# Attention units with 128 keys: the scaling of the probabilities goes from VectorE to ScalarE

## The chip, the cores and the metric

One core of a Trainium2 chip. The kernel is one program, written by hand for each engine with semaphores between them. The metric is device time in microseconds (us) of one execution; the median of three runs of the kernel before is 2493.39 us (2491.39 to 2496.73).

## What is computed

Two transformer blocks one after the other, on 256 tokens of width 1024 in float32. Their mixers hold several attentions, all of them with the same softmax. Cut to what the change touches:

```python
def masked_softmax(s, mask):
    s = jnp.where(mask, s, NEG_INF)
    m = jnp.max(s, axis=-1, keepdims=True)
    p = jnp.where(mask, jnp.exp(s - m), 0.0)
    return p / jnp.maximum(jnp.sum(p, axis=-1, keepdims=True), TINY)
...
    # nsa_attention, 16 heads of 64: three attentions, each weighted by a gate per token and head
    o = gc[..., 0:1] * o_c + gc[..., 1:2] * o_s + gc[..., 2:3] * o_w
```

DSA and MoBA (8 heads of 64 each) and MLA (8 heads of 192, values of 128) have no gate. All of these are causal: the first 128 queries see at most 128 keys, the second 128 queries see up to 256. The memory attention (4 heads of 128) has 256 keys for every query.

## The kernel before, in words

Everything lies in SBUF (on-chip memory) in one big array (`arena` in the profile); weights come by DMA in slabs through a ring, and TensorE multiplies them with activations of 256 tokens. Between the big products stand the attention stages. The list `units` holds their work: one unit is a pair of heads (e = 0, 1) for one block of 128 queries (`qt`), with `nk` keys. The order is: MoBA (8 units), DSA (8), memory attention (4), NSA in three kinds of 16 units each (kind 0 with 15 compressed keys, kinds 1 and 2 with 128 or 256 keys), memory attention (4), MLA (8): 80 units. In MoBA, DSA, NSA kinds 1 and 2, and MLA the even units have 128 keys and the odd ones 256; 28 units have 128 keys, and 16 of these, those of NSA, have a gate.

A unit u goes through these steps, in a software pipeline written out once per engine (`attention` in the block of each engine; the loop index is i):

- TensorE `scores(u)` writes query times key to PSUM (`pair`, a pair of banks). In round i it does `scores(i + 1)`, then `between` (in MoBA/DSA and NSA one or two products of the memory attention's weights, `memory_products`), then `values(i - 3)`, then `turn_p(i - 2)`. In MLA, where nothing is between, `turn_p(i - 2)` stands ahead of `values(i - 3)`.
- VectorE `maxima(u)`: L1699 scales and masks the scores (PSUM to `pb` in SBUF) and frees the scores' bank, L1704 takes the negative maximum. L1699 waits for the scores of u and, since `pb` has three places, for `turn_p(u - 3)` (semaphore `pT_done`).
- ScalarE `probs(u)`, L1215: the exponential of each head with the row sum as a second output (an ACTIVATE and an ACTIVATION_READ_ACCUMULATOR for each head).
- VectorE `weights(u)`: L1710 takes the reciprocal of the two sums, then a TENSOR_SCALAR for each head multiplies the probabilities by it (L1714), or by it and by the gate (L1716).
- TensorE `turn_p(u)`, L831: transposes the probabilities to the one PSUM bank there is for this (in MLA there are two), so it also waits for `copy_p(u - 1)`.
- ScalarE `copy_p(u)`: L1227 for 256 keys, L1230 for 128, takes the transposed probabilities to SBUF.
- TensorE `values(u)` (under L543, the line of every ordinary matmul), then VectorE `outputs(u)`, L1726 (adds to what is there) or L1728.

Each engine runs its own instructions in order, so a wait holds up everything behind it. ScalarE's order in a round is `probs(i)`, `copy_p(i - 2)`, `between` (L1207, `memory_out`: a copy of a finished memory product, for which TensorE waits before it starts the next group). VectorE's order is `maxima(i)`, `weights(i - 1)`, `outputs(i - 4)`, and in MoBA a round of the top-k of DSA (L2039, L2042).

Of the kernel before, what the change touches and what calls it, by code (L numbers as in the profile page):

```python
# [8 lines left out]
ALU = mybir.AluOpType  # L9
ACT = mybir.ActivationFunctionType  # L10
# [3 lines left out]
P = 128  # L14
# [4 lines left out]
HD = 64  # L19
# [186 lines left out]
def build(nc, stream, adaw_d, crow_d, xin, memin, cols_d, rows_d, gmrows_d, gmws_d, cmpw_d, consts_d, pos_d, out_d):  # L206
    with ExitStack() as ctx:
# [17 lines left out]
        stat = sb("stat", [P, 7, 56])  # L225
# [15 lines left out]
        def sem(name):  # L241

            if name not in sems:
                sems[name] = ctx.enter_context(nc.semaphore(name))
            return sems[name]
# [96 lines left out]
        def nsa_units(kind):  # L342
            def make(pair, qt):
                g = pair // 2
                gate = [stat[:, 5 + qt, 3 * (2 * pair + e) + kind:3 * (2 * pair + e) + kind + 1] for e in range(2)]
                if kind == 0:
                    return dict(qt=qt, nk=N_CMP, scale=HD ** -0.5, mask=cmpmask[:, qt, 0:N_CMP], gate=gate, dv=HD,
                                s=[[(qT[HD * e:HD * e + HD, pair, qt * P:qt * P + P],
                                     kcmpT[HD * e:HD * e + HD, g * N_CMP:g * N_CMP + N_CMP])] for e in range(2)],
                                v=[[vcmp[0:N_CMP, g, :]]] * 2, out=oT[:, pair, qt * P:qt * P + P], add=False)  # L350
                nk = P * (qt + 1)
                keys, v0 = (kT, NS_VS) if kind == 1 else (kwT, NS_VW)
                return dict(qt=qt, nk=nk, scale=HD ** -0.5, mask=causal[:, qt, 0:nk], gate=gate, dv=HD,
                            s=[[(qrT[HD * e:HD * e + HD, pair, qt * P:qt * P + P],
                                 keys[HD * e:HD * e + HD, g, 0:nk])] for e in range(2)],
                            v=[[tm[:, kt, v0 + HD * g:v0 + HD * g + HD] for kt in range(qt + 1)]] * 2,
                            out=oT[:, pair, qt * P:qt * P + P], add=True)
            return make
# [24 lines left out]
        U_MEM1 = add_units("mem1", 2, mem_unit)  # L383
        U_MLA = add_units("mla", 4, mla_unit)


        def pair_jobs(c0, n, dst, d0):

# [150 lines left out]
        def _(pe):  # L539
# [265 lines left out]
            def attention(first, last_unit, between=None):  # L805
                behind = 1 if between is None else 0

                def scores(u):
                    un = units[u]
                    if u >= 2:  # L810
                        pe.wait_ge(sem("scores_read"), u - 1)
                    for e in range(2):
                        parts = un["s"][e]
                        for i, (q, k) in enumerate(parts):
                            ins = mm(spair[u % 2][:, e, 0:un["nk"]], q, k, i == 0, i == len(parts) - 1)
                    ins.then_inc(sem("scores_done"), 1)

                def turn_p(u):
                    un = units[u]
                    nk = un["nk"]  # L820
                    pe.wait_ge(sem("p_done"), u + 1)
                    if u > behind:
                        pe.wait_ge(sem("pT_copied"), u - behind)
                    tb = banks[TB[u % 2 * behind]]
                    if nk < P:
                        for e in range(2):
                            ins = mm(tb[0:nk, e * TOK:e * TOK + P], pb[:, u % 3, e, 0:nk], ident, True, True)
                    else:
                        for e in range(2):
                            for kt in range(nk // P):  # L830
                                ins = nc.tensor.transpose(tb[:, (2 * e + kt) * P:(2 * e + kt + 1) * P],  # L831
                                                          pb[:, u % 3, e, kt * P:kt * P + P], ident)
                    ins.then_inc(sem("pT_done"), 1)

                def values(u):
                    un = units[u]
                    kp = min(un["nk"], P)
                    pe.wait_ge(sem("pT_copied"), u + 1)
                    if u >= 2:
                        pe.wait_ge(sem("o_read"), u - 1)  # L840
                    ob = banks[OB[u % 2]]
                    for e in range(2):
                        vs = un["v"][e]
                        out = ob[HD * e:HD * e + HD, 0:P] if un["dv"] == HD else ob[:, e * P:e * P + P]
                        for kt, v in enumerate(vs):
                            ins = mm(out, v, pT[0:kp, u % 2, 2 * e + kt, :], kt == 0, kt == len(vs) - 1)
                    ins.then_inc(sem("o_done"), 1)

                scores(first)
                for i in range(first, last_unit + 3):  # L850
                    if i + 1 < last_unit:
                        scores(i + 1)
                    if between is not None:
                        between(i - first)
                    if behind and first <= i - 2 < last_unit:
                        turn_p(i - 2)
                    if i - 3 >= first:
                        values(i - 3)
                    if not behind and first <= i - 2 < last_unit:
                        turn_p(i - 2)  # L860
# [274 lines left out]
        def _(act):  # L1135
# [73 lines left out]
            def attention(first, last_unit, between=None):  # L1209
                def probs(u):  # L1210
# [5 lines left out]
                                                   accum_out=att_s[:, u % 3, 1, e:e + 1])  # L1216
                    ins.then_inc(sem("exp_done"), 1)

                def copy_p(u):
                    un = units[u]  # L1220
                    nk = un["nk"]
                    act.wait_ge(sem("pT_done"), u + 1)
                    if u >= 2:
                        act.wait_ge(sem("o_done"), u - 1)
                    tb = banks[TB[0 if between is not None else u % 2]]
                    if nk == TOK:
                        ins = nc.scalar.copy(pT[:, u % 2, :, :].rearrange("p a q -> p (a q)"), tb[:, :])  # L1227
                    else:
                        kp = min(nk, P)
                        ins = nc.scalar.copy(pT[0:kp, u % 2, 0:4:2, :],  # L1230
                                             tb[0:kp, :].rearrange("p (a q) -> p a q", a=4)[:, 0:4:2, :])
                    ins.then_inc(sem("pT_copied"), 1)

                for i in range(first, last_unit + 2):
                    if i < last_unit:
                        probs(i)
                    if i - 2 >= first:
                        copy_p(i - 2)
                    if between is not None:
                        between(i - first)  # L1240
# [223 lines left out]
        def _(dve):  # L1464
# [222 lines left out]
            def attention(first, last_unit, between=None):  # L1687
# [18 lines left out]
                def weights(u):  # L1706
                    un = units[u]
                    dve.wait_ge(sem("exp_done"), u + 1)
                    r = att_s[:, u % 3, 2, :]
                    link(V.reciprocal(r, att_s[:, u % 3, 1, :]))  # L1710
                    for e in range(2):
                        p = pb[:, u % 3, e, 0:un["nk"]]
                        if un["gate"] is None:
# [799 lines left out]
```

## Time and profile before

| | |
|---|---|
| median of 3 runs | 2493.39 us (2491.39 to 2496.73) |
| the profiled execution | 2495.09 us, its span 2493.3 us |
| TensorE busy | 2409.8 us, 97% of the span |
| VectorE busy | 1620.8 us, 65% |
| ScalarE busy | 528.7 us, 21% |
| mean granted TensorE clock | 0.994 of full speed |

The busy time of an engine is summed over the span. A profile also follows back a chain of work from the last instruction; a chain entry names the engine that the end was waiting for at that moment. In the rows below PE is TensorE (its times are modelled from starts, and neighbouring instructions overlap by about 0.07), PEld its weight loads, DVE VectorE, ACT ScalarE. A duration is from start to end; the next instruction of the same engine may start some 0.09 us ahead of that end when it depends on nothing.

### The profile page before, as it was taken

The numbers are of one execution on the slowest core, as the hardware profiler recorded it, in microseconds if no ns is written. First come the engines' busy times: TensorE is split into PE (matmuls) and PEld (weight loads), VectorE is DVE, ScalarE is ACT, GpSimd is POOL, SyncE is SP. The second block draws the span as 40 slices with busy tenths as digits, with TensorE's granted clock in tenths as the row PEclk, the third lists the DMA queues.
The fourth block names the chain that finished last, engine by engine and source line by source line (L and its number), as shares of the span: only waits on it lengthen the run. The fifth ranks groups of instructions, "written<-read, shape, count | busy, mean of one in ns | idle before, by whom it ended". The sixth has DMA issues, their size and how long they took to land.

```text
span 2493.3 us, 40490 instructions
## 1 busy us (share of the span) xinstructions
PE 2409.8 (97%) x15728; PEld 2041.9 (82%) x15728; DVE 1620.8 (65%) x3373; ACT 528.7 (21%) x1346; POOL 111.0 (4%) x212
## 2 busy tenths in 40 slices
PE   7998999999989999999999999999999999999997
PEld 4476999655669996789998699997789996789997
DVE  4765887448558872427985469864849982426873
ACT  2232010126320102102211332112232202103210
POOL 0000001000000010000110001100001110000000
PEclk9999999999999999999999999999999999999999
DMA  6323557531126574536876258773238774434442
GB/s 232 113 103 131 206 206 258 202 113 35 68 98 258 206 260 162 177 119 217 296 270 223 85 196 292 263 270 136 93 118 328 280 284 156 169 119 146 159 161 68
DMA packets 122363, 453.46 MB, mean 182 GB/s; under 512 B 13776, under 2 KB 13904, under 8 KB 121680
## 3 DMA queue, kind: packets, MB, share of 16 engines
q1 hardware_dynamic: 92880, 338.24, 38.1%
q0 software_dynamic: 29312, 112.80, 12.5%
q8 instruction: 125, 2.05, 0.3%
q14 instruction: 46, 0.38, 0.1%
HBM read 449.93 MB, written 1.05 MB: 181 GB/s over the span
## 4 chain that ended last, share of the span: by engine, by line
PE 79%; DVE 13%; DMA 3%; issue 3%; ACT 2%; DVEq 0%; SPq 0%; POOL 0%; ACTq 0%
PE pair L543 56%; PE bank L543 22%; DMA adat<-adaw_dram 3%; DVE adat L1847 2%; DVE att_s L1704 1%; DVE arena L1791 1%; DVE arena L1699 1%; DVE arena L1578 1%; DVE arena L1584 1%; DVE rstd L1479 1%; DVE arena L1580 1%; DVE h L1482 1%; PE bank L831 1%; DVE arena L1793 1%; PE bank L774 0%
## 5 line engine op out<-in xcount | busy, mean ns | idle before, releaser
L543 PE MATMUL pair<-h,ring 128*128 128x256 f32 (+1 forms) x3424 | 639.8, 346 | 10.4 <-issue 5.6
L543 PEld LDWEIGHTS pair<-h,ring 128*128 128x128 f32 x3424 | 568.4, 191 | 71.9 <-issue 8.0
L543 PE MATMUL pair<-arena,ring 128*128 128x128 f32 (+1 forms) x2476 | 387.8, 316 | 4.5 <-issue 3.6
L543 PEld LDWEIGHTS pair<-arena,ring 128*128 128x128 f32 x2476 | 354.9, 193 | 31.8 <-issue 4.9
L543 PE MATMUL pair<-ring,h 128*128 128x512 f32 (+1 forms) x768 | 326.2, 582 | 3.0 <-DVE h L1482 3.0
L543 PEld LDWEIGHTS bank<-arena 128*128 128x128 f32 (+2 forms) x2584 | 275.5, 186 | 46.3 <-issue 19.9
L543 PE MATMUL bank<-arena 128*128 128x128 f32 (+2 forms) x2584 | 297.9, 280 | 15.5 <-ACT arena L1227 9.9
L543 PE MATMUL pair<-arena 128*128 128x128 f32 (+6 forms) x2530 | 300.3, 284 | 10.0 <-ACT arena L1199 3.6
L543 PEld LDWEIGHTS pair<-arena 128*128 128x128 f32 (+4 forms) x2530 | 262.4, 185 | 43.3 <-issue 22.7
L543 PEld LDWEIGHTS pair<-ring,h 128*128 128x128 f32 x768 | 142.5, 191 | 168.3 <-issue 159.6
L1847 DVE CUSTOM_DVE_ANT_0 adat<-adat,crow,cols 128x1024 f32<-128x1024 f32 x192 | 244.2, 1278 | 51.0 <-DMA adat<-adaw_dram 50.9
L543 PE MATMUL bank<-arena,ring 128*128 128x128 f32 x1912 | 227.7, 276 | 0.2 <-DVE arena L1802 0.2
L543 PEld LDWEIGHTS bank<-arena,ring 128*128 128x128 f32 x1912 | 220.7, 192 | 1.3 <-DVE arena L1757 0.4
L500 POOL DMA_DIRECT2D adat<-adaw_dram x192 | 101.4, 528 | 1438.0 <-DVE mod L1847 1429.3
L1641 DVE COPY arena<-pair 128x512 f32<-128x512 f32 (+2 forms) x52 | 33.9, 654 | 188.3 <-PE pair L543 188.2
L1582 DVE TENSOR_TENSOR arena<-ring 128x512 f32<-128x512 f32 (+5 forms) x104 | 85.8, 828 | 34.0 <-PE bank L543 23.3
L1578 DVE TENSOR_TENSOR arena<-ring 128x512 f32<-128x512 f32 (+5 forms) x104 | 85.5, 826 | 30.1 <-DMA ring<-stream_dram 30.1
L1510 DVE SCALAR_TENSOR_TENSOR x<-pair,fin,x 128x256 f32<-128x256 f32 (+1 forms) x40 | 17.2, 430 | 128.7 <-PE pair L543 128.6
L1178 ACT ACTIVATE h<-x 128x256 f32<-128x256 f32 x84 | 32.6, 413 | 308.3 <-DVE x L1510 144.6
L1584 DVE TENSOR_TENSOR arena<-ring,arena 128x512 f32<-128x512 f32 (+5 forms) x104 | 86.2, 832 | 5.0 <-PE pair L543 0.8
L1580 DVE TENSOR_TENSOR arena<-arena,ring 128x512 f32<-128x512 f32 (+5 forms) x104 | 86.2, 832 | 4.2 <-PE bank L543 0.8
L1215 ACT ACTIVATE arena<-arena,att_s 128x256 f32<-128x256 f32 (+2 forms) x160 | 67.5, 423 | 56.8 <-DVE att_s L1704 53.3
(231 smaller groups left out, 2163.9 us busy)
## 6 DMA issues: line engine op xcount, KB each, us to landing
ring<-stream_dram SPq DMA_DIRECT2D x638, 512.0 KB, 4.4
adat<-adaw_dram POOLq DMA_DIRECT2D x192, 512.0 KB, 4.9
arena<-gmrows_dram POOLq DMA_DIRECT2D x2, 2560.0 KB, 11.1
arena<-cmpw_dram POOLq DMA_DIRECT2D x1, 2112.0 KB, 9.4
x<-x_in_dram SPq DMA_DIRECT2D x2, 512.0 KB, 4.7
arena<-mem_in_dram SPq DMA_DIRECT2D x1, 1024.0 KB, 12.7
arena<-gmws_dram POOLq DMA_DIRECT2D x2, 512.0 KB, 13.1
out_dram<-h POOLq DMA_DIRECT2D x2, 512.0 KB, 3.8
```

What stands on the lines that cost most here:

```text
L500: pool.dma_start(adat[:, n % ADA_RING, :], adaw_d[n]).then_inc(sem(f"ada_in{n % ADA_RING}"), 16)
L543: return nc.tensor.matmul(out, lhsT, rhs, start=start, stop=stop)
L831: ins = nc.tensor.transpose(tb[:, (2 * e + kt) * P:(2 * e + kt + 1) * P], pb[:, u % 3, e, kt * P:kt * P + P], ident)
L1178: nc.scalar.activation(h[:, k, :], x[:, k, :], ACT.Square).then_inc(sem("sq_done"), 1)
L1215: ins = nc.scalar.activation(p, p, ACT.Exp, bias=att_s[:, u % 3, 0, e:e + 1], accum_out=att_s[:, u % 3, 1, e:e + 1])
L1479: V.reciprocal(rstd[:, 1, cols], rstd[:, 0, cols]).then_inc(sem("rstd_read"), 1)
L1578: ins = V.tensor_tensor(s[0], part(2, a, b), part(3, a, b), ALU.add)
L1580: ins = V.tensor_tensor(s[1], s[0], part(0, a, b), ALU.subtract)
L1582: ins = V.tensor_tensor(s[2], part(0, a, b), part(2, a, b), ALU.subtract)
L1584: ins = V.tensor_tensor(s[3], part(1, a, b), s[1], ALU.subtract)
L1641: V.tensor_copy(dst(n % 2, n // 2 * 512, w), banks[g % 2][:, 0:w]).then_inc(sem("freed_dve"), 1)
L1847: V.tensor_tensor_reduce(out=w, in0=w, in1=crow[:, :], scale=1.0, scalar=col(f"ada_b{i}", t), op0=ALU.mult, op1=ALU.add, accum_out=mod[:, ...
```

## The change

For units with exactly 128 keys (not for those with 15) VectorE stops after the factor: the reciprocal, and in NSA one TENSOR_TENSOR of two columns that multiplies in both gates. ScalarE does the two multiplications itself (`scaled`), between `probs(i)` and `copy_p(i - 2)`, for unit i - 1. TensorE's transpose waits for the semaphore of whichever engine scaled the unit.

```diff
+                at = 3 * 2 * pair + kind
+                gates = stat[:, 5 + qt, at:at + 4:3]
...
+        done = {"p_done": 0, "p_scaled": 0}
+        for un in units:
+            un["by"] = "p_scaled" if un["nk"] == P else "p_done"
+            done[un["by"]] += 1
+            un["p"] = done[un["by"]]
...
# TensorE, turn_p
-                    pe.wait_ge(sem("p_done"), u + 1)
+                    pe.wait_ge(sem(un["by"]), un["p"])
...
# ScalarE
+                def scaled(u):
+                    un = units[u]
+                    act.wait_ge(sem("p_factor"), un["p"])
+                    for e in range(2):
+                        p = pb[:, u % 3, e, 0:P]
+                        ins = nc.scalar.activation(p, p, ACT.Identity, scale=att_s[:, u % 3, 2, e:e + 1])
+                    ins.then_inc(sem("p_scaled"), 1)
...
                     if i < last_unit:
                         probs(i)
+                    if first <= i - 1 < last_unit and units[i - 1]["by"] == "p_scaled":
+                        scaled(i - 1)
                     if i - 2 >= first:
                         copy_p(i - 2)
...
# VectorE, weights
-                    link(V.reciprocal(r, att_s[:, u % 3, 1, :]))
+                    ins = V.reciprocal(r, att_s[:, u % 3, 1, :])
+                    if un["by"] == "p_scaled":
+                        if un["gate"] is not None:
+                            link(ins)
+                            ins = V.tensor_tensor(r, r, un["gates"], ALU.mult)
+                        ins.then_inc(sem("p_factor"), 1)
+                        return
+                    link(ins)
```

ScalarE in NSA, two units of 256 keys and the one of 128 between them, before (att_s holds maxima, sums and factors; `max_done` comes from L1704, `pT_done` and `o_done` from TensorE):

```order
L1215 ACTIVATE arena,att_s<-arena,att_s 128x256 [waits max_done]
L1215 ACTIVATE arena,att_s<-arena,att_s 128x256
L1227 COPY arena<-bank 128x512 [waits o_done,pT_done]
L1215 ACTIVATE arena,att_s<-arena,att_s 128x128 [waits max_done]
L1215 ACTIVATE arena,att_s<-arena,att_s 128x128
L1230 COPY arena<-bank 128x2x128 [waits o_done,pT_done]
```

The same place in the changed kernel (L1223 is L1215 before, L1243 is L1227, L1246 is L1230):

```order
L1223 ACTIVATE arena,att_s<-arena,att_s 128x256 [waits max_done]
L1223 ACTIVATE arena,att_s<-arena,att_s 128x256
L1232 ACTIVATE arena<-arena,att_s 128x128 [waits p_factor]
L1232 ACTIVATE arena<-arena,att_s 128x128
L1243 COPY arena<-bank 128x512 [waits o_done,pT_done]
L1223 ACTIVATE arena,att_s<-arena,att_s 128x128 [waits max_done]
L1223 ACTIVATE arena,att_s<-arena,att_s 128x128
L1246 COPY arena<-bank 128x2x128 [waits o_done,pT_done]
```

Two activations now stand between the exponentials of a 256-key unit and the copy of the 256-key unit before it; nothing is added in the other half of the round.

VectorE in NSA, one unit of 128 keys and its surroundings, before:

```order
L1699 SCALAR_TENSOR_TENSOR arena<-pair,cst 128x512 [waits pT_done,scores_done]
L1704 TENSOR_REDUCE att_s<-arena 128x2 [waits scores_read]
L1710 RECIPROCAL att_s<-att_s 128x2 [waits exp_done]
L1716 TENSOR_SCALAR arena<-arena,att_s,stat 128x128 [waits dve_chain]
L1716 TENSOR_SCALAR arena<-arena,att_s,stat 128x128
L1726 TENSOR_TENSOR arena<-bank,arena 128x128 [waits o_read,o_done]
```

and in the changed kernel (L1717 is L1699 before, L1722 is L1704, L1728 is L1710, L1751 is L1726):

```order
L1717 SCALAR_TENSOR_TENSOR arena<-pair,cst 128x512 [waits pT_done,scores_done]
L1722 TENSOR_REDUCE att_s<-arena 128x2 [waits scores_read]
L1728 RECIPROCAL att_s<-att_s 128x2 [waits exp_done]
L1732 TENSOR_TENSOR att_s<-att_s,stat 128x2 [waits dve_chain]
L1751 TENSOR_TENSOR arena<-bank,arena 128x128 [waits o_read,o_done]
```

The two multiplications of 128 columns are gone, and one of two columns is there; in MoBA, DSA and MLA not even that. Number and order of TensorE's instructions, of GpSimd's and of the DMA issues are the same in both kernels.

## Rows read from the trace of the kernel before

**Rows 1.** The page: busy time by engine, and the chain that ended last

```profile
PE 2409.8 (97%) x15728; PEld 2041.9 (82%) x15728; DVE 1620.8 (65%) x3373; ACT 528.7 (21%) x1346; POOL 111.0 (4%) x212
...
PE 79%; DVE 13%; DMA 3%; issue 3%; ACT 2%; DVEq 0%; SPq 0%; POOL 0%; ACTq 0%
```

**Rows 2.** Windows: stretch and its length, busy time by engine (instructions), clock

```profile
112.00:133.00 21.00, 18.78 (x95) 9.12 (x93) 20.16 (x71) 9.41 (x32) 0.00 (x0) 1.00 0.09 38
...
582.00:650.00 68.00, 61.58 (x442) 34.62 (x440) 63.31 (x191) 44.47 (x158) 0.00 (x0) 0.99 0.10 32
...
650.00:655.00 5.00, 3.31 (x19) 1.82 (x17) 0.96 (x4) 2.24 (x3) 0.00 (x0) 0.50 0.00 0
...
240.00:250.00 10.00, 6.79 (x52) 6.47 (x53) 9.65 (x26) 2.16 (x4) 0.00 (x0) 1.00 0.11 34
```

**Rows 3.** Timeline of VectorE in NSA: start us, duration us, what

```profile
607.67 0.69 DVE L1699 SCALAR_TENSOR_TENSOR arena<-pair,cst 128x512 f32<-128x512 f32 x1
608.40 0.69 DVE L1704 TENSOR_REDUCE att_s<-arena 128x2 f32<-128x512 f32 x1
609.00 0.15 DVE L1710 RECIPROCAL att_s<-att_s 128x2 f32<-128x2 f32 x1
609.19 0.60 DVE L1716 TENSOR_SCALAR arena<-arena,att_s,stat 128x128 f32<-128x128 f32 x2
609.71 0.28 DVE L1726 TENSOR_TENSOR arena<-bank,arena 128x128 f32<-128x128 f32 x1
...
611.87 0.69 DVE L1699 SCALAR_TENSOR_TENSOR arena<-pair,cst 128x512 f32<-128x512 f32 x1
```

**Rows 4.** Timeline of ScalarE in the same round

```profile
609.12 0.51 ACT L1215 ACTIVATE arena<-arena,att_s 128x256 f32<-128x256 f32 x1 [1.14 <-DVE att_s L1704]
...
610.12 0.56 ACT L1227 COPY arena<-bank 128x512 f32<-128x512 f32 x1
```

**Rows 5.** Timeline of TensorE in the same round

```profile
610.73 0.67 PE L543 MATMUL bank<-arena 128*64 128x128 f32 x8 [0.41 <-ACT arena L1227]
611.33 0.44 PE L831 MATMUL bank<-cst,arena 128*128 128x128 f32 x2
```

**Rows 6.** Timeline of VectorE: L1699 of the units 17, 23 and 47 of NSA

```profile
581.70 0.69 DVE L1699 SCALAR_TENSOR_TENSOR arena<-pair,cst 128x512 f32<-128x512 f32 x1 [0.93 <-PE bank L543]
...
595.04 0.69 DVE L1699 SCALAR_TENSOR_TENSOR arena<-pair,cst 128x512 f32<-128x512 f32 x1 [0.73 <-PE bank L831]
...
645.57 0.69 DVE L1699 SCALAR_TENSOR_TENSOR arena<-pair,cst 128x512 f32<-128x512 f32 x1
```

**Rows 7.** ScalarE: groups by shape, and eight activations back to back in the timeline

```profile
L1191 ACT ACTIVATE h<-h,mod 128x128 f32<-128x128 f32 x128 | 39.1, 388 | 22.5 <-DVE h L1482 22.5
...
949.68 2.45 ACT L1191 ACTIVATE h<-h,mod 128x128 f32<-128x128 f32 x8 [1.41 <-DVE h L1482]
...
L1275 ACT ACTIVATE arena<-arena,cols 128x256 f32<-128x256 f32 x80 | 43.7, 593 | 96.6 <-DVE arena L1631 96.6
...
L1284 ACT ACTIVATE arena<-arena 128x256 f32<-128x256 f32 x88 | 36.7, 417 | 31.4 <-DVE arena L1793 31.3
...
L1186 ACT ACTIVATE h<-x 128x128 f32<-128x128 f32 x56 | 16.6, 306 | 91.1 <-DVE x L1510 53.6 <-DVE x L1509 37.6
```

**Rows 8.** Timeline of VectorE in MoBA, a unit of 128 keys without a gate

```profile
109.07 0.48 DVE L1714 TENSOR_SCALAR arena<-arena,att_s 128x128 f32<-128x128 f32 x2
109.47 0.74 DVE L2039 MAX8 arena<-arena 128x8 f32<-128x256 f32 x2
```

**Rows 9.** Timeline of TensorE: its waits for ScalarE in MoBA, DSA and MLA

```profile
117.92 1.98 PE L543 MATMUL bank<-ring,arena 128*128 128x512 f32 x4 [1.61 <-ACT arena L1207]
...
142.85 1.13 PE L543 MATMUL bank<-ring,arena 128*128 128x256 f32 x4 [0.37 <-ACT arena L1207]
...
153.21 0.66 PE L543 MATMUL bank<-arena 128*64 128x128 f32 x8 [1.34 <-ACT arena L1227]
...
1420.91 1.16 PE L543 MATMUL bank<-arena 128*128 128x128 f32 x8 [0.57 <-ACT arena L1227]
```

More of the change, by code:

```diff
@@ L352, in make @@
                 keys, v0 = (kT, NS_VS) if kind == 1 else (kwT, NS_VW)
-                return dict(qt=qt, nk=nk, scale=HD ** -0.5, mask=causal[:, qt, 0:nk], gate=gate, dv=HD,
+                return dict(qt=qt, nk=nk, scale=HD ** -0.5, mask=causal[:, qt, 0:nk], gate=gate, gates=gates, dv=HD,
                             s=[[(qrT[HD * e:HD * e + HD, pair, qt * P:qt * P + P],
```

## The prediction, made before the changed kernel was run

> **What bounds the kernel now.** I read the page first [rows 1]: TensorE is busy for 97% of the span and holds 79% of the chain that ended last, VectorE 13%, ScalarE 2%. So over the whole span only a stage in which TensorE waits can give or take time. The change touches three stages (MoBA and DSA, NSA kinds 1 and 2, MLA), so next I took windows of them [rows 2]. In NSA from 582 to 650 us VectorE is busy 63.31 of 68.0 us, TensorE 61.58, ScalarE 44.47. Read by busy time alone, VectorE limits there, and the change takes work from it. That reading has to be checked against the timeline, because several engines wait for each other in turn.
>
> The timeline shows a closed loop, and its length is the length of the round (two units, one of 256 keys and one of 128). Start with L1699 of a 256-key unit i at 607.67 [rows 3]. 0.73 later L1704 starts (608.40) and it ends at 609.09. ScalarE, idle for 1.14 before, starts the exponentials of i at 609.12 [rows 4] and has both heads' done 1.00 later; at 610.12 it starts the copy L1227 of the unit i - 2, which takes 0.56 and ends at 610.68. TensorE has stood idle for 0.41 for that copy [rows 5]. Its eight matmuls of `values(i - 2)` start at 610.73 and the transpose of unit i - 1 follows at 611.33, 0.60 later, and lasts 0.44 to 611.77. L1699 of unit i + 2 waits for just this transpose (its place in `pb` comes free by it) and starts at 611.87 [rows 3]. The sum: 0.73 + 0.69 + 0.03 + 1.00 + 0.56 + 0.05 + 0.60 + 0.44 + 0.10 = 4.20, and 611.87 - 607.67 = 4.20. Over twelve rounds, L1699 moves from 595.04 to 645.57 [rows 6], 4.21 a round. VectorE's multiplications are **not in this loop**: they run while ScalarE does the exponentials. And ScalarE, the engine with the most spare time, is in it with 1.56 us.
>
> **The change part by part.** *What VectorE loses.* The pair L1716 of 128 columns takes 0.52 from its start to the next one's (609.19 to 609.71) [rows 3], without a gate 0.40 (109.07 to 109.47) [rows 8]. With a gate a two-column operation comes in; its nearest row is L1710, two columns, 0.15 long, 0.19 to a dependent successor [rows 3]. So VectorE gains 0.33 to 0.4 a round. In NSA that is worth nothing, since the loop doesn't pass there: the gain lengthens VectorE's own waits for the transpose. The cover that hides this work is ScalarE's exponentials.
>
> *What ScalarE gets.* Two activations of 128 columns, SBUF to SBUF, with a scale for each partition. No row shows that form. The nearest is L1191, 128 columns with one per-partition operand (the bias): 388 ns long on the mean, and eight back to back last 2.45 us [rows 7], so they start (2.45 - 0.388) / 7 = 0.295 apart. Bounds: below, no charge for the operand, L1186 at 0.306 long, some 0.21 apart, 0.43 for the pair. Above, the operand costs all that scale and bias cost together, L1275 against L1284, 593 - 417 = 176 ns [rows 7], so 0.39 apart, 0.78 for the pair. I take 0.59 for the pair, the row that has one such operand and the same shape; 0.43 and 0.78 are kept for the range. Its wait costs nothing: the factor is ready 0.3 us after L1704's end, and the exponentials ahead of the scaling last 1.00.
>
> *Where it lies.* The order of the instructions shows it: the pair stands behind the exponentials of the 256-key unit and ahead of its L1227 copy, once a round. Just that copy is the step for which TensorE waits. So the loop becomes 4.20 + 0.59 = 4.79. Queued behind the pair are L1227, then the next exponentials; TensorE's `values`, the transpose and with it VectorE's next L1699 all wait for them. The transpose of the scaled unit itself comes later than all that, so its own semaphore is not the one that ends last. The floor by TensorE's work, 61.58 us over sixteen rounds, about 3.8, stays below. No DMA is issued differently, and no table load comes in: the order of both kernels has 45 of them.
>
> *The sum for NSA.* Between L1699 of unit 17 at 581.70 and of unit 23 at 595.04 there are three rounds of 13.34 together [rows 6], longer than three loops would be, since TensorE still has the products of 512 columns and the units of kind 0 in them; of these three I count one and a half. Then twelve rounds in full, and the last copy in the drain of the stage once: 14.5 x 0.59 = **8.6 us**.
>
> *MoBA and DSA.* At 117.92 TensorE waits 1.61 for L1207 [rows 9], which stands behind one added pair (+0.59) and behind exponentials that start some 0.4 earlier as VectorE has one multiplication less on the way: +0.2. From there TensorE is nearly full (18.78 of 21.0 [rows 2]) and VectorE's earlier finish pays for the pair. In DSA, TensorE waits 0.37 for L1207 at 142.85 and 1.34 for L1227 at 153.21 [rows 9]; each has the pair ahead of it: 2 x 0.59. Sum **1.2 us**, taking the 0.2 as inside the slack in between.
>
> *MLA.* The transpose of a unit doesn't wait behind the values there, and TensorE has longer products of its own; the one wait that I find for a copy with the pair ahead of it is in the drain, 0.57 for L1227 at 1420.91 [rows 9]: **0.6 us**. The memory attentions and NSA kind 0 are untouched.
>
> Together 8.6 + 1.2 + 0.6 = 10.4 us. The profiled execution would go from 2495.09 to 2505.5; it stands 1.7 above the median, so for the median I forecast 2493.4 + 10.3, **2503.7 us**.
>
> The Trainium skill, page "ScalarE: Activation LUTs", section "Rules for kernel authors", speaks against such a move in general: multiplications belong on VectorE. It reasons from the speed of an element on either engine. By engine time alone the change would cost 0.59 - 0.52 for each of the 16 gated units and 0.59 - 0.40 for each of the 12 others, 3.4 us, if both engines were always waited for; no row supports that, and by the loop the place in ScalarE's queue counts and not the difference of speeds.
>
> **The rivals.** *VectorE is the bound after all (faster).* For it: 63.31 of 68.0 us busy in NSA [rows 2], 93%. Then each of the fourteen rounds that it sets gets shorter by 0.4, down to TensorE's floor of 3.8, and the pair hides in ScalarE's 1.14 of idle time before each exponential [rows 4]: 14 x 0.4 = 5.6, so 2487.8. Against it: the loop's sum closes at 4.20 without VectorE's multiplications, and the idle time of ScalarE lies ahead of the exponentials, not between them and the copy. It decides if the exponentials could start earlier by as much as the pair takes, 0.59. 6%.
>
> *The pair is hidden (no change).* TensorE's wait for the copy is filled from products elsewhere and the price is near 0.2 instead of 0.59; about 2494 to 2497. For it: only that ScalarE has 23 of 68 us free. 6%.
>
> *The clock falls (slower still).* TensorE's share of work falls from 3.8 of 4.21 to 3.8 of 4.79, 80%. In the drain of the stage the granted clock is 0.50, its lower level of 1.2 GHz, after longer waits [rows 2]; but from 240 to 250 us TensorE was busy 6.79 of 10 at full clock [rows 2], and the new waits are each below 1 us. If it fell for the whole of NSA, 3.8 us of work would become about 7 a round, 14 x 2.3 = 32 more, 2536; one lapse of a round costs 2 to 3 and stays in the range. The Trainium skill's page "TensorE: Matmul & The Clock Gate", Part 1, says as much of the direction: the gate passes fewer pulses when the engine was idle enough of late. 6% for a loss that leaves the range.
>
> That the change does nothing is excluded by the order of the instructions: 56 multiplications are gone from one engine and stand on the other.
>
> **How the numbers follow.** Forecast 82%, and 6% for each rival. The pair's bounds scale the 17.5 places where it counts: 0.43 gives 7.5 us, 2500.9, and 0.78 gives 13.7, 2507.1. The runs of before scatter by -2.0 and +3.3 around their median [the table of times], and a drain can meet the other clock level, 2 us either way. So 2499.0 to 2508.5. Since 0.2% (5.0 us) is about what a measurement of this kernel can tell from no change, slower means above 2498.4: the forecast and the clock case, with a part of the forecast lost at the low end, 0.87. Within 0.2%: the hidden pair and that part, 0.07. Faster: 0.06.
>
> **What would show it.** In NSA, L1717 (L1699 before) of the 256-key units every 4.8 us, with an idle time ahead of it that TensorE's transpose ends, and VectorE busy some 3.5 of 4.8 us (63.31 over 16 rounds is 3.9, less 0.60, plus 0.15). ScalarE's pair of L1232 right behind the exponentials, 0.6 us from start to the copy. TensorE idle some 1.0 us a round for L1243. DSA's last waits 0.6 longer, all products outside these stages unchanged. Wrong if the round is 4.2 or less, if the exponentials of the 256-key units start earlier against the transpose than now, or if the granted clock in NSA isn't full.

## The result, and the profile after

The changed kernel takes 2507.39 us in the median of 6 runs (2499.86 to 2509.23), the kernel before 2493.38 (2491.39 to 2499.88) in runs beside them. The ratio is 1.0047, with a 95% interval of 1.003 to 1.0064: **slower**, by 11.7 us as the ratio has it. The forecast was 2503.7 in a range of 2499.0 to 2508.5. The profiled execution took 2505.75 us, its span is 2503.9, 10.6 more than before; the forecast for it was 2505.5. That last agreement is partly luck, as the account by stages shows below.

The page of the changed kernel, busy time by engine and the chain that ended last:

```profile
PE 2411.5 (96%) x15728; PEld 2041.4 (82%) x15728; DVE 1609.5 (64%) x3333; ACT 543.3 (22%) x1402; POOL 111.0 (4%) x212
...
PE 77%; DVE 13%; DMA 4%; ACT 3%; issue 2%; DVEq 0%; SPq 0%; POOL 0%; ACTq 0%
```

Against [rows 1], VectorE has 40 instructions and 11.3 us less, ScalarE 56 instructions and 14.6 us more. So these two engines together have 3.3 us more of work, and the span is 10.6 us longer. The step of the chain that tells something is ScalarE's share, 2% to 3%: it has become a longer piece of the path.

The round in NSA, first VectorE's timeline (start us, duration us, what; in brackets the idle time before and what ended it):

```profile
609.05 0.69 DVE L1717 SCALAR_TENSOR_TENSOR arena<-pair,cst 128x512 f32<-128x512 f32 x1 [0.86 <-PE bank L839]
609.78 0.69 DVE L1722 TENSOR_REDUCE att_s<-arena 128x2 f32<-128x512 f32 x1
...
610.57 0.16 DVE L1732 TENSOR_TENSOR att_s<-att_s,stat 128x2 f32<-128x2 f32 x1
...
613.84 0.69 DVE L1717 SCALAR_TENSOR_TENSOR arena<-pair,cst 128x512 f32<-128x512 f32 x1 [1.06 <-PE bank L839]
```

ScalarE's timeline of the same round:

```profile
610.50 0.51 ACT L1223 ACTIVATE arena<-arena,att_s 128x256 f32<-128x256 f32 x1 [1.14 <-DVE att_s L1722]
...
611.50 0.68 ACT L1232 ACTIVATE arena<-arena,att_s 128x128 f32<-128x128 f32 x2
612.08 0.56 ACT L1243 COPY arena<-bank 128x512 f32<-128x512 f32 x1
```

TensorE's timeline of the same round:

```profile
612.70 0.67 PE L551 MATMUL bank<-arena 128*64 128x128 f32 x8 [1.00 <-ACT arena L1243]
613.29 0.44 PE L839 MATMUL bank<-cst,arena 128*128 128x128 f32 x2
```

It is the loop of [rows 3], [rows 4] and [rows 5] with one link more. From the exponentials at 610.50 to the end of both heads at 611.50 are 1.00, as before; then the pair L1232 holds the copy back until 612.08, 0.58 later; the copy ends at 612.64, the values start at 612.70, the transpose at 613.29, 0.59 later, lasts 0.44, and L1717 starts at 613.84. Together 613.84 - 609.05 = 4.79. VectorE was idle for 1.06 and waited for the transpose (L839).

Windows of the changed kernel (stretch and its length, busy time by engine with instructions, clock, DMA share, GB/s):

```profile
112.00:133.00 21.00, 18.76 (x103) 9.60 (x102) 19.18 (x62) 11.32 (x38) 0.00 (x0) 1.00 0.08 23
...
582.00:650.00 68.00, 56.84 (x403) 31.50 (x402) 51.89 (x158) 47.91 (x175) 0.00 (x0) 1.00 0.10 32
...
660.00:670.00 10.00, 9.44 (x36) 7.64 (x37) 5.95 (x9) 1.52 (x2) 0.00 (x0) 0.68 0.35 123
```

In NSA VectorE falls from 63.31 of 68 us to 51.89 and TensorE from 61.58 [rows 2] to 56.84, since fewer rounds fit into the stretch. The granted clock stays full through the stage; behind its drain it is 0.68 from 660 to 670.

**The account by stages.** These are the first operations of VectorE in each stage, before:

```profile
105.06 0.42 DVE L1699 SCALAR_TENSOR_TENSOR arena<-pair,cst 128x256 f32<-128x256 f32 x1 [0.50 <-PE pair L543]
...
211.83 0.69 DVE L1697 TENSOR_SCALAR arena<-pair 128x512 f32<-128x512 f32 x1 [2.29 <-PE pair L543]
...
710.87 0.69 DVE L1697 TENSOR_SCALAR arena<-pair 128x512 f32<-128x512 f32 x1 [2.29 <-PE pair L543]
...
1399.44 0.43 DVE L1699 SCALAR_TENSOR_TENSOR arena<-pair,cst 128x256 f32<-128x256 f32 x1 [2.65 <-PE pair L543]
```

and of the changed kernel, with L1717 of the NSA units 17, 23 and 47 between them (those of before are [rows 6]):

```profile
102.43 0.42 DVE L1717 SCALAR_TENSOR_TENSOR arena<-pair,cst 128x256 f32<-128x256 f32 x1 [0.50 <-PE pair L551]
...
210.32 0.69 DVE L1715 TENSOR_SCALAR arena<-pair 128x512 f32<-128x512 f32 x1 [2.29 <-PE pair L551]
...
580.50 0.69 DVE L1717 SCALAR_TENSOR_TENSOR arena<-pair,cst 128x512 f32<-128x512 f32 x1 [0.92 <-PE bank L551]
...
594.70 0.69 DVE L1717 SCALAR_TENSOR_TENSOR arena<-pair,cst 128x512 f32<-128x512 f32 x1 [0.73 <-PE bank L839]
...
652.10 0.69 DVE L1717 SCALAR_TENSOR_TENSOR arena<-pair,cst 128x512 f32<-128x512 f32 x1 [0.86 <-PE bank L839]
...
718.22 0.69 DVE L1715 TENSOR_SCALAR arena<-pair 128x512 f32<-128x512 f32 x1 [2.29 <-PE pair L551]
...
1410.27 0.43 DVE L1717 SCALAR_TENSOR_TENSOR arena<-pair,cst 128x256 f32<-128x256 f32 x1 [2.64 <-PE pair L551]
```

| stretch | before | after | more | forecast |
|---|---|---|---|---|
| start of MoBA | 105.06 | 102.43 | -2.63 | 0 |
| MoBA and DSA, to the memory attention | 106.77 | 107.89 | +1.12 | 1.2 |
| from there to NSA unit 17 | 369.87 | 370.18 | +0.31 | 0 |
| NSA units 17 to 23 | 13.34 | 14.20 | +0.86 | 0.9 |
| NSA units 23 to 47, 12 rounds | 50.53 | 57.40 | +6.87 | 7.1 |
| from unit 47 to the second memory attention | 65.30 | 66.12 | +0.82 | 0.6 |
| from there to MLA | 688.57 | 692.05 | +3.48 | 0 |
| MLA, to the last values behind L1227 or L1232 | 21.47 | 22.04 | +0.57 | 0.6 |
| from there to the end | 1072.39 | 1071.59 | -0.80 | 0 |

The MLA row runs from the stage's first L1699 or L1717 to the values at 1420.91 before [rows 9] and at 1432.31 after (shown further down). The three changed stages give 1.12 + 0.86 + 6.87 + 0.82 + 0.57 = 10.2 us of the 10.4 forecast. The unchanged stretches gave -2.6, +3.8 and -0.8, which nearly cancel in this execution.

### The profile page after: what moved, and what is told of

It reads as the page before. It is cut to its first block, busy times and chain, and to the rows that moved or that the text cites. A ratio compares the mean times of both kernels' runs of the same rounds, so it can differ in the third digit from the quotient of the medians.

```text
span 2503.9 us, 40506 instructions
## 1 busy us (share of the span) xinstructions
PE 2411.5 (96%) x15728; PEld 2041.4 (82%) x15728; DVE 1609.5 (64%) x3333; ACT 543.3 (22%) x1402; POOL 111.0 (4%) x212
## 4 chain that ended last, share of the span: by engine, by line
PE 77%; DVE 13%; DMA 4%; ACT 3%; issue 2%; DVEq 0%; SPq 0%; POOL 0%; ACTq 0%
PE pair L551 54%; PE bank L551 22%; DMA adat<-adaw_dram 3%; DVE adat L1872 2%; DVE arena L1816 1%; ACT arena L1223 1%; PE bank L839 1%; DVE arena L1596 1%; DVE arena L1602 1%; DVE att_s L1722 1%; DVE arena L1598 1%; DVE rstd L1497 1%; DVE arena L1818 1%; DVE arena L1717 1%; DVE h L1500 1%
## 5 line engine op out<-in xcount | busy, mean ns | idle before, releaser
L551 PE MATMUL pair<-h,ring 128*128 128x256 f32 (+1 forms) x3424 | 640.0, 346 | 11.3 <-issue 6.6
L1223 ACT ACTIVATE arena<-arena,att_s 128x256 f32<-128x256 f32 (+2 forms) x160 | 67.5, 423 | 48.0 <-DVE att_s L1722 47.2
```

The costliest lines, as they stand in the source:

```text
L551: return nc.tensor.matmul(out, lhsT, rhs, start=start, stop=stop)
L1223: ins = nc.scalar.activation(p, p, ACT.Exp, bias=att_s[:, u % 3, 0, e:e + 1], accum_out=att_s[:, u % 3, 1, e:e + 1])
```

## The experiments

**The changed kernel once more, beside the others.** No edit.

> The changed kernel itself, to see how much of the difference of the medians (14.0 us) is the change. Theory (the pair of activations lies in the loop of NSA, and in front of the copies in MoBA/DSA and MLA): the three stages take 10.2 us more in the trace (1.12, 8.53, 0.57), so the medians should lie 9 to 12 apart here; what was above that is scatter of the runs. Rival: something outside the three stages got slower for good (DMA or clock): 13 to 15 again, and the trace would show the same offset between the stages again (+3.5 us from the memory attention of block 2 to MLA).

Measured: 2505.88 us (2500.12 to 2511.7, 6 runs), and 2494.63 for the kernel before (29 runs); the ratio is 1.0053 (1.0038 to 1.0067). Its profiled execution took 2500.12. The round was 4.787, MoBA and DSA 1.14 longer than before, NSA from unit 17 to the second memory attention 137.41 against 129.17, so 8.24 longer. But the stretch from there to MLA took 688.05, 0.5 less than before. So the +3.5 of that stretch in the first trace was scatter and not the change.

**The pair behind the copy.**

```diff
-                    if first <= i - 1 < last_unit and units[i - 1]["by"] == "p_scaled":
-                        scaled(i - 1)
                     if i - 2 >= first:
                         copy_p(i - 2)
+                    if first <= i - 1 < last_unit and units[i - 1]["by"] == "p_scaled":
+                        scaled(i - 1)
```

> The changed kernel with the pair of scalings one place later in ScalarE's order, behind copy_p(i - 2). The same instructions and the same engine times. Theory (place in the queue): the copy is not delayed, and the scaling is done 1.19 us after the copy's start, just when the transpose is due (0.56 + 0.05 + 0.60 = 1.21), so the round of NSA is back at 4.20 to 4.25 us instead of 4.79, and the time is 8 to 9 us below the changed kernel; MoBA/DSA and MLA keep their 1 to 2 us, as the memory copies stand behind both: 2494 to 2496 if before is at 2493.4. Rival (ScalarE's extra work costs as such, or the scaling's own semaphore holds the transpose): the round stays at 4.7 or more, no gain over the changed kernel.

Measured: 2497.65 us (2493.02 to 2506.12, 12 runs), ratio 1.0014 (1.0001 to 1.0027). The round is 4.215. ScalarE's and TensorE's timelines:

```profile
614.40 0.56 ACT L1243 COPY arena<-bank 128x512 f32<-128x512 f32 x1
614.86 0.69 ACT L1232 ACTIVATE arena<-arena,att_s 128x128 f32<-128x128 f32 x2
```

```profile
615.01 0.66 PE L551 MATMUL bank<-arena 128*64 128x128 f32 x8 [0.32 <-ACT arena L1243]
```

The same two activations, as long as in the changed kernel, run beside the values now (615.01), and the round has its old length. So the loss in NSA is a matter of place in ScalarE's order, not of the work moved. The NSA stage, from unit 17 to the second memory attention, was 128.08, 1.1 less than before.

In the other stages the pair costs something behind the copy too. In MoBA and DSA ScalarE's L1215 (the copy of a memory product, L1207 before) stands behind both. The L1717 of the last DSA unit comes 46.21 us after the first one of MoBA, against 45.09 before and 45.63 with the pair ahead of the copy, all at full clock. From there to the memory attention this execution lost 2.6 us more, with a granted clock of 0.62 from 155 to 160 us and 0.69 from 160 to 165, where the kernel before had 1.00. In MLA the transpose of the drain waits 1.99 for the pair itself, and the values behind it start 22.33 us after the stage's first L1717 in place of 21.47. That fits a median that is still 3.0 us above the kernel before; the time is a little above the 2494 to 2496 that were expected.

**No scaling.** ScalarE's pair is left out, TensorE waits for the factor instead. The probabilities of the units with 128 keys are left unmultiplied.

```diff
-                    pe.wait_ge(sem(un["by"]), un["p"])
+                    pe.wait_ge(sem("p_factor" if un["by"] == "p_scaled" else "p_done"), un["p"])
...
-                    if first <= i - 1 < last_unit and units[i - 1]["by"] == "p_scaled":
-                        scaled(i - 1)
```

> The changed kernel without the pair on ScalarE: the probabilities of the 28 units with 128 keys are not multiplied at all, VectorE makes the factor only. Theory (VectorE's multiplications are not in the loop): round of NSA 4.20, the same as before, although VectorE has 0.4 us less to do in it; the whole 0 to 2 us below before (a little in MoBA, nothing in NSA). Rival (VectorE bounds NSA): round 3.8 to 3.85, 6 to 7 us below before.

Measured: 2494.25 us (2491.45 to 2505.79, 12 runs), ratio 1.0002 (0.9989 to 1.0014). VectorE's timeline:

```profile
612.59 0.69 DVE L1715 SCALAR_TENSOR_TENSOR arena<-pair,cst 128x512 f32<-128x512 f32 x1 [0.48 <-PE bank L839]
...
616.79 0.69 DVE L1715 SCALAR_TENSOR_TENSOR arena<-pair,cst 128x512 f32<-128x512 f32 x1 [0.27 <-PE bank L839]
```

VectorE has the smaller work of the changed kernel, and ScalarE has nothing more. The round is 4.20 here, 4.211 over twelve, exactly that of the kernel before. That is the test of the first rival: taking the multiplications from VectorE is worth **nothing** in a round of NSA; the gain becomes its own waits of 0.48 and 0.27 for the transpose. The stage as a whole was 1.2 us shorter (127.93 against 129.17), 1.0 of it in the drain behind unit 47, where this execution had a granted clock of 1.00 from 640 to 650 us against 0.91 before. MoBA and DSA gained 0.6 (106.15).

**One activation ahead of the copy, one behind it.** `scaled(i - 1, 0)` stands ahead of `copy_p(i - 2)`, `scaled(i - 1, 1)` behind it.

> The changed kernel with the pair divided: the first head's scaling ahead of copy_p(i - 2), the second one's behind it. Theory: half the price in the loop, round of NSA 4.20 + 0.29 = 4.49 us; the second scaling then ends 0.9 us after the copy's start, ahead of the transpose. Rival (the semaphore p_scaled or a fixed cost of the wait makes the delay): 4.79 as with both ahead, or 4.2.

Measured: one run, 2505.26 us, and a round of 4.494, half way between 4.215 and 4.783. (The time as a whole is that of the changed kernel all the same; this single run had a mean clock of 0.991.) ScalarE's timeline:

```profile
615.63 0.39 ACT L1232 ACTIVATE arena<-arena,att_s 128x128 f32<-128x128 f32 x1
615.92 0.56 ACT L1244 COPY arena<-bank 128x512 f32<-128x512 f32 x1
```

**The pair twice.** Ahead of the real pair stand two more activations of the same form into a buffer that nobody reads.

```diff
+                    for e in range(2):
+                        nc.scalar.activation(rstd[:, e, 0:P], pb[:, u % 3, e, 0:P], ACT.Identity,
+                                             scale=att_s[:, u % 3, 2, e:e + 1])
```

> The changed kernel with a second pair of the same two activations in front of the first, which writes to a place that nobody reads (rstd); the result is the same. Theory: everything that ScalarE puts ahead of the copy is paid in full, round of NSA 4.79 + 0.59 = 5.38 us and some 8.5 us more than the changed kernel; two more in MoBA/DSA and MLA. Rival (a slack or a wait was filled by the first pair): less than 5.2. If TensorE's clock falls with its share of work (3.8 of 5.4), the round is longer than 5.4.

Measured: one run, 2536.21 us. ScalarE's timeline:

```profile
627.59 0.68 ACT L1231 ACTIVATE rstd<-arena,att_s 128x128 f32<-128x128 f32 x2
628.17 0.68 ACT L1235 ACTIVATE arena<-arena,att_s 128x128 f32<-128x128 f32 x2
628.76 0.56 ACT L1246 COPY arena<-bank 128x512 f32<-128x512 f32 x1
```

VectorE's timeline:

```profile
625.14 0.69 DVE L1720 SCALAR_TENSOR_TENSOR arena<-pair,cst 128x512 f32<-128x512 f32 x1 [1.76 <-PE bank L839]
...
630.51 0.69 DVE L1720 SCALAR_TENSOR_TENSOR arena<-pair,cst 128x512 f32<-128x512 f32 x1 [1.65 <-PE bank L839]
```

This round is 5.37, and so, within 0.01, are four others of the twelve from unit 23 to unit 47. With the other kernels there is now a straight line: 0, 1, 2 and 4 activations ahead of the copy give 4.215, 4.494, 4.783 and 5.37, that is +0.28, +0.57 and +1.16, or 0.29 for each. **The loop is shown**, and so is its price. But a round was that short only while the granted clock was full. Windows of this kernel:

```profile
585.00:610.00 25.00, 22.13 (x141) 10.79 (x140) 17.45 (x60) 17.01 (x65) 0.00 (x0) 1.00 0.00 1
610.00:690.00 80.00, 64.91 (x360) 36.13 (x360) 44.98 (x137) 51.10 (x177) 0.00 (x0) 0.74 0.08 27
```

and the same group of TensorE, scores of 256 keys, in two of its rounds:

```profile
621.29 1.23 PE L551 MATMUL pair<-arena 64*128 64x256 f32 x4
...
626.46 0.70 PE L551 MATMUL pair<-arena 64*128 64x256 f32 x4
```

In the round of the first row the clock was at its lower level for a time (the four matmuls take 1.23 in place of 0.70), and it took 7.23 us; the second row lies in the round of 5.37. The seven longer rounds of the twelve took 5.55 to 7.54, the mean of all twelve is 6.09, and the mean clock from 610 to 690 is 0.74. That is the rival of the falling clock. It didn't come with one pair, and did with two.

**Four places for the probabilities, from the kernel before.** What closes the loop is that L1699 of unit i + 2 waits for the transpose of i - 1. A fourth place takes that away; `rstd`, the norms' buffer, is free in these stages and serves as the fourth.

```diff
-        att_s = sb("att_s", [P, 3, 3, 2])
+        att_s = sb("att_s", [P, 4, 3, 2])
...
+        pbs = [pb[:, 0], pb[:, 1], pb[:, 2], rstd]
...
# everywhere: pb[:, u % 3, ...] becomes pbs[u % 4][:, ...], att_s[:, u % 3, ...] becomes att_s[:, u % 4, ...]
...
# VectorE, maxima
-                    if u >= 3:
-                        dve.wait_ge(sem("pT_done"), u - 2)
+                    if u >= 4:
+                        dve.wait_ge(sem("pT_done"), u - 3)
```

> The kernel before with four places for the probabilities instead of three (the fourth lies in rstd, which no attention uses), so that L1699 of unit u waits for the transpose of unit u - 4. Theory (the loop closes through the place in pb): without that edge the round of NSA falls from 4.21 to what VectorE needs in order, about 4.0 to 4.1; 2 to 3 us less than before. Rival (the loop isn't the bound, VectorE's sequence is): 4.2 remains, no change.

Measured: 2490.6 us (2481.93 to 2500.53, 12 runs), ratio 0.9985 (0.9971 to 1.0). The round is 4.132. VectorE's timeline:

```profile
614.34 0.68 DVE L1700 SCALAR_TENSOR_TENSOR arena<-pair,cst 128x512 f32<-128x512 f32 x1
...
618.20 0.29 DVE L1727 TENSOR_TENSOR arena<-bank,arena 128x128 f32<-128x128 f32 x1
618.40 0.68 DVE L1700 SCALAR_TENSOR_TENSOR rstd<-pair,cst 128x512 f32<-128x512 f32 x1
```

L1700 starts 0.20 after the start of the instruction ahead of it, L1727. In the kernel before this was 0.33, up to the L1699 at 611.87 [rows 3]:

```profile
611.54 0.28 DVE L1726 TENSOR_TENSOR arena<-bank,arena 128x128 f32<-128x128 f32 x1
```

So VectorE had waited 0.13 a round for the place in `pb`, too little for a bracket in the view, and now it does not wait: it is the limit at last. These two rows are 4.06 apart. The 4.132 is a mean over twelve rounds of which the first, with products of 512 columns in it, takes 4.93 and each of the others 4.05 to 4.06. In the kernels with three places the long round (5.0 to 5.1) lies ahead of unit 23, so it is not in their means. The steady round therefore went from 4.21 to 4.06, and this is also how near VectorE stood to being the limit before: 0.15 us a round.

**The same from the changed kernel**, with the pair ahead of the copy as in the change.

> The changed kernel with four places for the probabilities instead of three. In this kernel the edge from the transpose of unit i - 1 to L1717 of unit i + 2 is gone, and with it the loop in which the pair lay. Theory: the round of NSA falls from 4.79 to about 4.0, below the 4.13 that VectorE's own sequence needed in the kernel before with four places, because VectorE has 0.4 less to do; the pair then costs almost nothing: 2489 to 2493 (before 2494.6). Rival (ScalarE's extra time is paid whatever the places are): round 4.5 or more, 2500 or more.

Measured: 2489.48 us (2483.43 to 2496.47, 12 runs), 2494.6 beside it for the kernel before (18 runs), ratio 0.9972 (0.9957 to 0.9987). The round is 3.954. With the place gone from the loop, the same change that cost 0.57 a round **saves 0.18** (4.132 to 3.954). VectorE's timeline, L1718 of the units 25 and 47:

```profile
597.01 0.68 DVE L1718 SCALAR_TENSOR_TENSOR arena<-pair,cst 128x512 f32<-128x512 f32 x1
...
639.53 0.69 DVE L1718 SCALAR_TENSOR_TENSOR rstd<-pair,cst 128x512 f32<-128x512 f32 x1
```

Over these eleven rounds, without the long first one, it is 3.87 against 4.06.

For the whole kernel this gain is not shown. The NSA stage from unit 17 to the second memory attention took 127.22 here and 126.80 in the kernel before with four places (129.17 with three): the rounds gave back 2.1 and the drain took 2.5 more. The values in it ran at the lower clock sooner, here first, and in the other kernel second:

```profile
643.85 1.13 PE L552 MATMUL bank<-arena 128*64 128x128 f32 x8 [1.28 <-ACT arena L1244]
```

```profile
645.80 0.67 PE L544 MATMUL bank<-arena 128*64 128x128 f32 x8 [1.36 <-ACT arena L1228]
```

MoBA and DSA were equal (106.01 and 106.05), and MLA paid 0.58. The medians of the two kernels, not taken side by side but each with 2494.6 for the kernel before beside it, are 1.1 us apart, and the intervals of their ratios overlap.

**The version that takes all of it together.** Four places, the pair behind the copy, and only the gated units (NSA) scaled by ScalarE:

```diff
-            un["by"] = "p_scaled" if un["nk"] == P else "p_done"
+            un["by"] = "p_scaled" if un["nk"] == P and un["gate"] is not None else "p_done"
```

> The version that should beat both: four places, the pair behind the copy, and the pair only in NSA (units with a gate), so that MoBA/DSA and MLA stay as before. Theory: round of NSA 3.95, TensorE nearly full (3.8), which is 0.26 x 14 = 3.6 us less than before in NSA, and MoBA/DSA 1 us less by the fourth place: 2488 to 2491. Rival (as for the run before): 2494 or more.

Measured: **2484.0 us** (2480.63 to 2497.22, 8 runs), ratio 0.9947 (0.9928 to 0.9966): faster than the kernel before, 10.6 us under it by the medians, and so faster than the changed kernel, which was above it both times. The round is 3.922, or 3.83 without the long first one, close to the 3.8 that the prediction took for TensorE's floor. The time is lower than the 2488 to 2491 that were expected, and not all of it is the edit. The NSA stage is 5.1 us shorter than before (124.10); the fourth place alone had given 0.7 in MoBA and DSA and 0.4 in MLA. That is 6.2, an estimate from traces of two versions. The mean clock of these eight runs was 0.9946, that of the 18 of the kernel before beside them 0.9924; at some 2 us for 0.001, as the last section has it, the 0.0022 between them stand for about the other 4.4. Whether the version brings the higher clock or met it by chance is open.

Windows of 590 to 640 us, of the kernel before:

```profile
590.00:640.00 50.00, 46.26 (x334) 26.05 (x332) 46.86 (x140) 33.38 (x118) 0.00 (x0) 1.00 0.13 43
```

Of the kernel before with four places:

```profile
590.00:640.00 50.00, 48.63 (x355) 27.66 (x354) 47.61 (x145) 34.74 (x123) 0.00 (x0) 1.00 0.12 43
```

Of the changed kernel, as it is:

```profile
590.00:640.00 50.00, 42.06 (x301) 23.68 (x302) 38.17 (x116) 34.55 (x125) 0.00 (x0) 1.00 0.13 43
```

And of this last version:

```profile
590.00:640.00 50.00, 49.67 (x362) 28.29 (x362) 45.67 (x142) 42.08 (x155) 0.00 (x0) 1.00 0.13 43
```

TensorE goes from 46.26 to 48.63 with the fourth place alone, down to 42.06 with the change alone, and to 49.67 of 50 in this version (49.41 in the one above): TensorE has next to no idle time left in these rounds. Between this version and the one above it lie 5.5 us of medians, of which the rounds explain 15 x 0.03 = 0.5. With four places the pair cost 0.58 in MLA and nothing in MoBA and DSA. The drain of NSA was 2.7 shorter in the traces, at a higher clock (0.92 against 0.69 from 640 to 650 us), and the runs had the higher mean clock (0.9946 against 0.9938); how the rest divides was not tried.

## Why the prediction was right

*The bound.* The reading that the busy time of VectorE (63.31 of 68) is not the limit held: without ScalarE's pair the round stayed at 4.21, though VectorE had less to do. It held by a small margin, since VectorE's own sequence needs 4.06. What set the round was the closed loop through the three places of `pb`, shown from both sides: more ahead of the copy lengthens it one for one, and a fourth place opens it.

*The pair.* Forecast 0.59 in bounds of 0.43 and 0.78; measured 0.58 (611.50 to 612.08), and 0.29 for one in the step from 4.215 to 4.494. The row with one per-partition operand of the same shape [rows 7] was the right one to take. The Trainium skill, page "ScalarE: Activation LUTs", section "What ACT_TABLE_LOAD costs", gives a formula for this form: 186 ns + 0.833 ns a column, 93 more for an operand by partition, and 93 of overlap between neighbours. An estimate by that section's formula for 128 columns is some 386 long and 293 apart. The trace agrees: a single one is 0.39 long, and the next instruction starts 0.29 after it (615.63 to 615.92 with one activation ahead of the copy).

*NSA.* 14.5 x 0.59 = 8.6 forecast, 8.55 measured in the first trace and 8.24 in the second. Within it the rounds were a little cheaper (0.57) and the drain of the first trace dearer (0.82 in place of 0.59; 0.45 in the second). That the stage met the forecast within 0.1 us in the first trace is in part luck: the drain alone differs by 0.37 between two traces of the same kernel.

*MoBA and DSA.* Forecast 1.2 as two waits of DSA; measured 1.12 and 1.14. TensorE's waits in these stages (L1215 of the changed kernel is L1207 before):

```profile
115.34 1.98 PE L551 MATMUL bank<-ring,arena 128*128 128x512 f32 x4 [1.66 <-ACT arena L1215]
...
140.76 1.13 PE L551 MATMUL bank<-ring,arena 128*128 128x256 f32 x4 [0.95 <-ACT arena L1215]
...
151.70 0.66 PE L551 MATMUL bank<-arena 128*64 128x128 f32 x8 [1.93 <-DVE arena L1753]
```

Against [rows 9] they are 1.61 to 1.66, 0.37 to 0.95 and 1.34 to 1.93. The first shows the pair paid by VectorE's earlier finish, the other two show it in full, 0.58 and 0.59. The run without scaling takes the two apart: with VectorE's earlier finish alone the stages are 0.62 shorter than before and the same three waits 1.08, 0.37 and 1.35, so the pair costs 3 x 0.58 = 1.74, and 1.74 - 0.62 = 1.12. The prediction reckoned that first place as 0.59 - 0.4 and left out the 0.2; with 0.62 in place of 0.4 nothing was left to leave out. The last row, with 1.93, is put down to VectorE's L1753, but the copy L1243 ends at 151.65 and the values start 0.05 later; that copy stands behind the pair.

*MLA.* The size was right (0.6 forecast, 0.57 measured) and **one step of the reasoning was wrong**. The prediction said that the transpose of the scaled unit itself comes too late to be the one that waits. In MLA `turn_p(i - 2)` stands ahead of `values(i - 3)`, and in the drain it does wait for it. TensorE in the kernel before:

```profile
1419.90 0.44 PE L831 MATMUL bank<-cst,arena 128*128 128x128 f32 x2 [0.39 <-DVE arena L1714]
```

and in the changed kernel:

```profile
1431.84 0.44 PE L839 MATMUL bank<-cst,arena 128*128 128x128 f32 x2 [1.51 <-ACT arena L1232]
...
1432.31 1.16 PE L551 MATMUL bank<-arena 128*128 128x128 f32 x8
```

Before, TensorE waited 0.39 for VectorE's multiplication and then 0.57 for L1227 [rows 9]; now it waits 1.51 once, for L1232, and the copy is done by the time the transpose is. 1.51 - 0.39 - 0.57 = 0.55. The number came out alike because either wait ends behind exponentials and pair on ScalarE.

*Signs that were forecast.* L1717 every 4.8 us with a wait for the transpose ahead: yes, 4.783. VectorE busy 3.5 a round: 38.17 us in 50 / 4.783 = 10.5 rounds are 3.65, a little more. TensorE's idle time for L1243, 1.0 a round: from round to round it is 0.48, 1.00 and 1.11 in turn, 0.86 in the mean; 1.0 was one wait taken for all.

*The rivals.* VectorE as the bound fell by the run without scaling, the hidden pair by the round itself, and the clock stayed at 1.00 in the rounds of NSA. The first rival's price was too high as well: the prediction itself has 0.33, not 0.4, for a gated unit, and once VectorE was the limit the whole change gave 0.19 a round (4.06 to 3.87), with TensorE busy for 49.41 of 50 us.

*The total.* The medians differ by 14.0 in the first comparison and 11.3 in the second, the stages by 10.2. The scatter comes with the granted clock. In the 29 runs of the kernel before, the 13 whose mean clock is at least 0.994 have a median of 2493.3, the 5 with at most 0.991 one of 2501.63. Over all runs of both comparisons, the changed kernel has a mean of 2506.1 at a clock of 0.9923 (12 runs), and the kernel before in its 29 runs 2495.4 at 0.9929: 10.8 apart, of which 0.0005 of clock at some 2 us for 0.001 is about 1. That leaves the 10 of the stages. The forecast of the median, 2503.7, stayed 2 to 4 us low; this scatter fits that. That the change itself makes low clocks more frequent, as drains lengthen, would fit too; twelve runs cannot decide it.

## What to carry to other kernels

Where several engines wait for each other in turn, write out one round of the loop as a sum of links until it closes on the measured period; the busy share of an engine (93% for VectorE here) says nothing about who sets that period, and work moved to the idlest engine costs its full length if its place in that engine's order is inside the loop. The remedy is then the order (behind the copy: 4.215) or the buffer that closes the loop (a fourth place: 4.132), and only once it is open does lighter work on the busy engine shorten the round (3.954, and 3.922 behind the copy). One more buffer turned this change's worth from a loss of 0.57 a round to a gain of 0.18. A gain in the rounds is not yet one of the kernel: here the drain, at the lower clock, took it back in the trace.

## What was not expected of the hardware

- Single executions spend whole stretches at the lower clock, also in stages that the edit does not touch. MLA took 18.4 us from its first unit to its last before and after the change (18.0 with four places), and some 26 in two other traces: in the run without scaling the granted clock was 0.50 from 1405 to 1415 us, in the last version 0.50 from 1400 to 1410. The profiled execution of that version took 2497.22 at a mean clock of 0.990, its other seven runs 2480.6 to 2487.3 at 0.994 to 0.996.
- 0.001 of a run's mean clock stands for 1.8 to 2.5 us, by a straight line through the runs of each kernel. At changes of this size it is worth reading beside every time.
- The second pair adds 0.59 to a round that the first had already lengthened by 0.57, and the clock began to drop to half in the rounds; with one pair it held there. The price jumps there: 2536.21 us in place of an estimated 2516 (the 2505.5 of the forecast and 17.5 x 0.59 more).
